# The first twenty microseconds of a two-layer decoder step: finer first loads, an earlier split of two weight units, a later norm, spare products

## The chip, the cores and the metric

The kernel runs on one core of one Trainium2 chip. A core has five engines that work side by side: TensorE multiplies matrices, VectorE (DVE in the profile) and ScalarE (ACT) do elementwise work, GpSimd (POOL) does elementwise work and starts DMAs, SyncE (SP) only starts DMAs. They meet through semaphores. SBUF is the memory on the core in which all tiles lie, PSUM the eight banks that TensorE writes. The metric is the device time of one execution in microseconds; the median of several executions is compared.

## The reference, cut to what matters

One step of a two-layer decoder trunk runs on 264 tokens (256 of a prompt, 8 samples). Only the beginning of layer 0 matters here:

```python
def rmsnorm(x, g):
    y = xf * lax.rsqrt(jnp.mean(xf * xf, axis=-1, keepdims=True) + NORM_EPS)
    return (y * g.astype(jnp.float32)).astype(x.dtype)
...
    z = jnp.einsum('bld,de->ble', hn, w_in)          # hn = rmsnorm(h, norm1), 1024 -> 2560
    u = z[..., :POOL_WIDTH]
    q, k, v, g = jnp.split(z[..., POOL_WIDTH:], 4, axis=-1)
    q = rope(...); k = rope(...) * (RET_HEAD_DIM ** -0.5)
```

After the two mixers follow an output projection, a feed-forward block (layer 0) or eight experts (layer 1), and a gated embedding.

## The kernel before, in words

**Operands in two parts.** Every fp32 product is made of three faster ones: an operand is split into a high part (rounded to the type fp32r, a copy by ScalarE) and a low part (the difference, by VectorE). `weights_first` issues xh*whi, xl*whi and xh*wlo (lines 727, 728, 729). So a weight "unit" (1024 rows x 256 columns, 1 MB, landing in the tile `raw`) must pass ScalarE (`hi`, line 1284, writes `whi`) and VectorE (`lo`, line 1575, writes `wlo`, in place of `raw`) before TensorE may use it. The input x (tile `h`, eight rows of 128 partitions x 264) passes ScalarE (`part`, line 1294: `xh`, scaled by the norm's gains) and VectorE (`finish`, line 1586: `xl`).

**Units and chunks.** w_in of layer 0 is ten units, numbered 0 to 9 (q, q, k, k, v, v, u, u, gate, gate). Each gives two "chunks" of 128 output columns, 24 products each, in a PSUM bank; chunk n is in bank n mod 4, banks 4 to 7 are for side steps. A chunk is scaled by the norm and taken out of PSUM by VectorE (`z_chunk`, lines 1721 and 1724), which counts `acc_free`; TensorE starts chunk n >= 4 only after `acc_free` has reached n - 3.

**The start.** Unit 0 comes in two halves (rows 0 to 511, 512 to 1023; line 661), unit 1 and unit 2 as a whole (line 649). `first_pair` runs a unit with both its chunks side by side, row block by row block, so that it can start with a part of the unit. The norm does not hold up the products: it is applied to the chunks afterwards. Its sum of squares is built from squares of x (five by GpSimd, line 2134, three by ScalarE, line 1460), four additions on GpSimd (line 2140) and four full fp32 products with a matrix of 1/1024 (line 869), which stand between the two halves of unit 1; then come a square root on ScalarE (line 1345) and a reciprocal on VectorE (line 1626).

**Order on the engines.** Each engine's program is written out by hand. `ahead(u)` splits unit u + 2 while unit u is multiplied. In layer 0 VectorE goes through j = 0 to 9 with: split of unit j + 2, then chunks 2j and 2j + 1.

**Rope.** As soon as chunk 3 (the last of q) has been taken out, GpSimd starts four DMAs that copy q with its halves swapped (line 2155, tile `sg`); the same for k after chunk 7 (tile `o`). After chunk 9 VectorE multiplies the swapped copy by the sine (line 1704) and adds (line 1706). The same for k follows chunk 11. After chunk 15 TensorE makes small side products, among them the scores of the retention (line 902), which VectorE scales (line 1644), and window sums for the samples (line 909); VectorE's rope steps, chunk copies and splits stand in its queue ahead of that scaling.

**Loads.** SP's queue carries the weights in the order of use; from unit 8 on a load waits until an older unit has been used (`unit_used`). Before that nothing holds the queue back. ScalarE's queue carries x (four DMAs, line 1448) and the 20 KB of gains ahead of it (line 1446).

## Time and profile before

| what | value |
|---|---|
| median of 3 executions | 892.67 us (892.07, 892.67, 894.69) |
| the profiled execution | 894.15 us, of which the span from first to last instruction is 892.4 us |
| TensorE busy | 869.1 us, 97% of the span |
| VectorE, ScalarE, GpSimd busy | 78%, 61%, 20% |
| granted TensorE clock, mean over the span | 0.993 |
| DMA | 237.59 MB, 266 GB/s |

Times in the rows further down are microseconds from the start of the span. The profiled execution lies 1.75 us above its span and inside the range of the three timed ones.

### The profile page before, as it was taken

To read this page: it belongs to the slowest core of one execution; us is meant where nothing else is said; L and a number is where in the kernel's file an instruction comes from. 1 tells how busy PE (TensorE), PEld (TensorE's weight loads), DVE (VectorE), ACT (ScalarE), POOL (GpSimd) and SP (SyncE) were. 2 spreads that over 40 slices of the span, in tenths; PEclk is the share of its full clock that TensorE was granted. 3 is DMA by queue.
4 is the path that set the end of the run, shared out by engine and by line. 5 is a ranking of instruction groups with operands and counts; after the bars stand their busy time and mean duration, and the time that the engine had idled before them with its cause. 6 is when DMAs were issued, how large, how long until landed. Compare 5 with 4: busy or idle time off the path is not lost.

```text
span 892.4 us, 14470 instructions
## 1 busy us (share of the span) xinstructions
PE 869.1 (97%) x5919; PEld 756.3 (85%) x5919; DVE 694.4 (78%) x797; ACT 541.2 (61%) x659; POOL 179.1 (20%) x190
## 2 busy tenths in 40 slices
PE   6999999999999999999999999999999999999995
PEld 6999899999999999999887777777777767777794
DVE  5796776564655588786869889898998989898976
ACT  5435654443435356355557878787778778876752
POOL 5456321100110012564411030003000100010012
PEclk9999999999999999999999999999999999999998
DMA  9993555545554554955339999999999999999801
GB/s 338 365 335 98 174 199 201 198 149 198 190 190 142 196 181 155 293 168 186 137 122 364 413 333 367 413 355 368 399 391 361 357 412 361 407 358 390 333 2 48
DMA packets 50739, 237.59 MB, mean 266 GB/s; under 512 B 4866, under 2 KB 8226, under 8 KB 42944
## 3 DMA queue, kind: packets, MB, share of 16 engines
q1 hardware_dynamic: 44672, 215.51, 64.7%
q0 software_dynamic: 5280, 20.04, 8.1%
q10 hardware_dynamic: 720, 1.10, 0.4%
q8 instruction: 47, 0.77, 0.3%
q14 instruction: 20, 0.16, 0.1%
HBM read 226.38 MB, written 9.63 MB: 264 GB/s over the span
## 4 chain that ended last, share of the span: by engine, by line
PE 78%; DVE 12%; ACT 4%; issue 3%; DMA 2%; POOL 1%; ACTq 0%; DVEq 0%; POOLq 0%
PE bank L727 12%; PE bank L728 11%; PE bank L729 11%; PE bank L1093 8%; PE bank L1094 8%; PE bank L1095 8%; DVE wlo L1575 5%; PE bank L1119 4%; PE bank L1118 4%; PE bank L1120 4%; ACT whi L1284 2%; DMA raw<-in_moe_w_down 1%; PE bank L854 1%; DMA o<-qk 1%; PE bank L1051 1%
## 5 line engine op out<-in xcount | busy, mean ns | idle before, releaser
L1575 DVE TENSOR_TENSOR wlo<-raw,whi 128x1408 fp32r<-128x1408 f32 (+2 forms) x292 | 466.9, 1633 | 96.1 <-ACT whi L1284 95.9
L1284 ACT ACTIVATE whi<-raw 128x1408 fp32r<-128x1408 f32 (+2 forms) x292 | 392.4, 1377 | 145.7 <-PE bank L729 82.3
L727 PE MATMUL bank<-xh,whi 128*128 128x264 f32 x672 | 194.6, 290 | 9.0 <-DVE xl L1586 8.2
L728 PE MATMUL bank<-xl,whi 128*128 128x264 f32 x672 | 192.3, 286 | 0.0
L729 PE MATMUL bank<-xh,wlo 128*128 128x264 f32 x672 | 192.1, 286 | 0.0
L1093 PE MATMUL bank<-whi,xeh 128*96 128x512 f32 (+1 forms) x384 | 143.8, 374 | 0.6 <-DVE hid L1879 0.6
L1094 PE MATMUL bank<-wlo,xeh 128*96 128x512 f32 (+1 forms) x384 | 143.6, 374 | 0.0
L1095 PE MATMUL bank<-whi,xel 128*96 128x512 f32 (+1 forms) x384 | 143.2, 373 | 0.0
L727 PEld LDWEIGHTS bank<-xh,whi 128*128 128x128 f32 x672 | 128.4, 191 | 10.4 <-DVE wlo L1966 8.2
L728 PEld LDWEIGHTS bank<-xl,whi 128*128 128x128 f32 x672 | 128.6, 191 | 0.1
L729 PEld LDWEIGHTS bank<-xh,wlo 128*128 128x128 f32 x672 | 127.9, 190 | 0.0
L1093 PEld LDWEIGHTS bank<-whi,xeh 128*96 128x96 f32 x384 | 62.0, 161 | 21.0 <-DVE wlo L1575 0.9
L1094 PEld LDWEIGHTS bank<-wlo,xeh 128*96 128x96 f32 x384 | 61.9, 161 | 19.1
L1095 PEld LDWEIGHTS bank<-whi,xel 128*96 128x96 f32 x384 | 61.8, 161 | 19.0
L727 PE MATMUL bank<-mh,whi 128*128 128x264 f32 x256 | 74.2, 290 | 0.6 <-DVE wlo L1575 0.5
L729 PE MATMUL bank<-mh,wlo 128*128 128x264 f32 x256 | 72.6, 284 | 0.0
L728 PE MATMUL bank<-ml,whi 128*128 128x264 f32 x256 | 72.6, 284 | 0.0
L1118 PE MATMUL bank<-whi,hh 128*96 128x512 f32 x176 | 70.4, 400 | 0.0
L1119 PE MATMUL bank<-wlo,hh 128*96 128x512 f32 x176 | 69.3, 394 | 0.0
L1120 PE MATMUL bank<-whi,hl 128*96 128x512 f32 x176 | 69.0, 392 | 0.0
L2110 POOL DMA_INDIRECT summed<-ys,to_row x6 | 8.7, 1456 | 225.6 <-ACT ys L1404 134.1
L727 PEld LDWEIGHTS bank<-mh,whi 128*128 128x128 f32 x256 | 48.2, 188 | 3.9 <-issue 1.9
(264 smaller groups left out, 1242.8 us busy)
## 6 DMA issues: line engine op xcount, KB each, us to landing
raw<-in_moe_w_gate SPq DMA_DIRECT2D x32, 1408.0 KB, 9.2
raw<-in_moe_w_up SPq DMA_DIRECT2D x32, 1408.0 KB, 9.5
raw<-in_moe_w_down SPq DMA_DIRECT2D x40, 1024.0 KB, 8.9
raw<-in_w_in SPq DMA_DIRECT2D x17, 1024.0 KB, 6.0
raw<-in_ffn_w_down SPq DMA_DIRECT2D x16, 704.0 KB, 4.2
raw<-in_ffn_w_gate SPq DMA_DIRECT2D x10, 1024.0 KB, 4.9
raw<-in_ffn_w_up SPq DMA_DIRECT2D x10, 1024.0 KB, 5.1
raw<-in_w_o SPq DMA_DIRECT2D x8, 1024.0 KB, 11.1
```

Of the source, the lines that this page charges most:

```text
L727: pe.matmul(out, w_hi, x_hi, start=start, stop=False)
L728: pe.matmul(out, w_hi, x_lo, start=False, stop=False)
L729: return pe.matmul(out, w_lo, x_hi, start=False, stop=stop)
L854: mm = pe.matmul(b[0:HD, a:a + 2], S[:, s, c, :], qm[:, s, c, :], start=True, stop=True)
L1093: pe.matmul(b, X, H[:, lo:lo + n], start=(k == 0), stop=False)
L1094: pe.matmul(b, X, L[:, lo:lo + n], start=False, stop=False)
L1095: mm = pe.matmul(b, Y, H[:, lo:lo + n], start=False, stop=(k == DC - 1))
L1118: pe.matmul(b, X, H[:, own], start=(i == 0), stop=False)
L1119: pe.matmul(b, X, L[:, own], start=False, stop=False)
L1120: mm = pe.matmul(b, Y, H[:, own], start=False, stop=(i == EC - 1))
L1284: act.activation(unit_hi(u), unit_raw(u), ACT.Copy).then_inc(hi_ready, 1)
L1575: dve.tensor_tensor(unit_lo(u), unit_raw(u), unit_hi(u).bitcast(F32), ALU.subtract).then_inc(lo_ready, 1)
```

## The change

It does the following, all of it in layer 0's first three units.

1. **Loads.** Unit 0 comes in quarters (two row blocks each), unit 1 in halves, on SP's queue. The gains move from the head of ScalarE's queue to the third place on SP's. x stays on ScalarE's queue, but its third and fourth DMA are issued after the loading of ScalarE's table and after the first quarter's high part. The load of unit 3 moves ahead of the large block of constants.
2. **Splits.** `hi_part` and `lo_part` split unit 0 by quarters and unit 1 by halves, each quarter ahead of the two rows of x that go with it. Units 2 and 3 are split right after unit 1: on ScalarE unit 2 ahead of six of the squares and unit 3 ahead of the square root, on VectorE both ahead of the reciprocal.
3. **Squares.** All eight are ScalarE's now; GpSimd only adds.
4. **Norm.** TensorE's four fp32 products of the norm move from the middle of unit 1 to the middle of unit 2 (between chunks 4 and 5).
5. **Banks.** Chunks 4, 5 and 6 go to banks 5, 6 and 7, and only from chunk 7 on does TensorE wait for `acc_free`.
6. **Spare products.** At the head of its program TensorE makes five full fp32 products of a tile of zeros into bank 7, 128 x 264 each, once that tile has been cleared; nobody reads them.

```diff
+        def main_bank(n):
+            return n + 1 if n in (4, 5, 6) else n % 4
...
-            first_rows(0, top_in)
-            first_rows(1, raw_landed[0])
+            first_rows(0, 0, top_in[0])
+            first_rows(0, 1, top_in[1])
+            sp.dma_start(gains[:, :, :], t["gains"]).then_inc(gains_in, 16)
+            first_rows(0, 2, top_in[2])
+            first_rows(0, 3, raw_landed[0])
+            first_rows(1, 0, top_in[3])
+            first_rows(1, 1, raw_landed[1])
+            load_rows(2, t["w_in_rows"][:, 512:768])
             sp.dma_start(const[:, 0:FIRST_CONST], t["const"][:, 0:FIRST_CONST]).then_inc(first_in, 16)
-            for u in range(1, 3):
-                load_rows(u, t["w_in_rows"][:, 256 * u:256 * (u + 1)])
+            dense(0, U_MIX[0] + 3, W_IN[3:4])
             sp.dma_start(const[:, FIRST_CONST:], t["const"][:, FIRST_CONST:]).then_inc(const_in, 16)
...
-                if at >= 4:
+                if at >= 7:
                     pe.wait_ge(acc_free, n - 3)
-                out = bank[at % 4][:, 0:T]
+                out = bank[main_bank(at)][:, 0:T]
...
-                if between is not None:
+                if between == (0, FIRST_NORM_IN):
+                    side_step(0, "norm1")
+                elif between is not None:
...
-                    if u and half == 0:
-                        side_step(0, "norm1")
...
+            pe.wait_ge(still, 1)
+            for _ in range(5):
+                pe.matmul(bank[7][:, 0:T], sq[:, 0, 0:P], sq[:, 0, :], start=True, stop=True)
...
-            act.dma_start(gains[:, :, :], t["gains"]).then_inc(gains_in, 16)
...
+            fetch_x(0)
+            fetch_x(1)
             act.wait_ge(still, 1)
             act.activation(rstd[0:1, 0:1], sq[0:1, 0, 0:1], ACT.Sqrt)
+            fetch_x(2)
+            for i in range(4):
+                hi_part(0, i)
+                if i == 0:
+                    fetch_x(3)
+                for m in (2 * i, 2 * i + 1):
+                    h_final(act, 0, m)
+                    part(0, m)
+            for m in range(2):
+                first_square(m)
+            for i in range(2):
+                hi_part(1, i)
+            ahead(0)
+            for m in range(2, DC):
+                first_square(m)
+            ahead(1)
...
+            for i in range(4):
+                lo_part(0, i)
+                for m in (2 * i, 2 * i + 1):
+                    finish(0, m)
+            for i in range(2):
+                lo_part(1, i)
+            ahead(0)
+            ahead(1)
...
-            for m in range(5):
-                pool.wait_ge(x_in[m // 2], 16)
-                pool.tensor_tensor(first[:, m, :], h[:, m, :], h[:, m, :], ALU.mult).then_inc(pool_step, 1)
-                steps += 1
-            pool.wait_ge(pool_step, steps)
             for m in range(0, DC, 2):
-                if m >= 4:
-                    pool.wait_ge(first_sq, m // 2 * 2 - 3)
+                pool.wait_ge(first_sq, m + 2)
```

How the order moves, at three places. First SP's queue at the start of the program, before and after (`raw` is the weights' landing tile, 128x4x256 a half of a unit, 128x2x256 a quarter, 128x8x256 a whole one):

```order
L661 DMA raw<-in_w_in_rows 128x4x256 x2
L686 DMA const<-in_const 128x129
L649 DMA raw<-in_w_in_rows 128x8x256 x2
L689 DMA const<-in_const 128x2709
L690 DMA pscale<-in_pscale 128x8
```

```order
L667 DMA raw<-in_w_in_rows 128x2x256 x2
L692 DMA gains<-in_gains 128x40
L667 DMA raw<-in_w_in_rows 128x2x256 x2
L667 DMA raw<-in_w_in_rows 128x4x256 x2
L655 DMA raw<-in_w_in_rows 128x8x256
L698 DMA const<-in_const 128x129
L645 DMA raw<-in_w_in 128x2048
L700 DMA const<-in_const 128x2709
```

The gains now follow two quarters; ahead of unit 2 (line 655) stand the same weights as before, without the first constants.

Second ScalarE at its first square root and the splits around it, before and after (line 1443, then 1463, is the high part of a piece of unit 0 or 1, line 1284, then 1303, of a whole unit; `first` holds the squares):

```order
L1443 ACTIVATE whi<-raw 128x1024 [waits raw_landed1] x2
L1460 ACTIVATE first<-h 128x264 x3
L1284 ACTIVATE whi<-raw 128x2048 [waits raw_landed2]
L1345 ACTIVATE rstd<-bank,const 128x264 [waits side_full,first_in]
L1284 ACTIVATE whi<-raw 128x2048 [waits unit_used,raw_landed3]
```

```order
L1468 ACTIVATE first<-h 128x264 x2
L1463 ACTIVATE whi<-raw 128x1024 [waits top_in3]
L1463 ACTIVATE whi<-raw 128x1024 [waits raw_landed1]
L1303 ACTIVATE whi<-raw 128x2048 [waits raw_landed2]
L1468 ACTIVATE first<-h 128x264 x6
L1303 ACTIVATE whi<-raw 128x2048 [waits unit_used,raw_landed3]
L1364 ACTIVATE rstd<-bank,const 128x264 [waits side_full,first_in]
```

Six squares now stand behind the split of unit 2, and the split of unit 3 has moved ahead of the square root.

Third VectorE around the reciprocal, before and after (line 1575, then 1609, is the low part of a unit; the rows `qk<-bank,rstd` are the chunks of q and k):

```order
L1575 TENSOR_TENSOR wlo<-raw,whi 128x2048 [waits hi_ready]
L1626 RECIPROCAL rstd<-rstd 128x264 [waits std_ready]
L1724 TENSOR_TENSOR qk<-bank,rstd 128x264 [waits acc_full,side_free]
L1724 TENSOR_TENSOR qk<-bank,rstd 128x264 [waits unit_used]
L1575 TENSOR_TENSOR wlo<-raw,whi 128x2048 [waits hi_ready]
L1724 TENSOR_TENSOR qk<-bank,rstd 128x264 [waits acc_full]
L1724 TENSOR_TENSOR qk<-bank,rstd 128x264 [waits unit_used]
```

```order
L1609 TENSOR_TENSOR wlo<-raw,whi 128x2048 [waits hi_ready] x2
L1660 RECIPROCAL rstd<-rstd 128x264 [waits std_ready]
L1758 TENSOR_TENSOR qk<-bank,rstd 128x264 [waits acc_full,side_free]
L1758 TENSOR_TENSOR qk<-bank,rstd 128x264 [waits unit_used]
L1758 TENSOR_TENSOR qk<-bank,rstd 128x264 [waits acc_full]
L1758 TENSOR_TENSOR qk<-bank,rstd 128x264 [waits unit_used]
```

The low part of unit 3 has moved from between chunks 1 and 2 to ahead of the reciprocal.

## Rows read from the trace of the kernel before

**Rows 1.** The page, busy time, share of the span and instructions of each engine

```profile
PE 869.1 (97%) x5919; PEld 756.3 (85%) x5919; DVE 694.4 (78%) x797; ACT 541.2 (61%) x659; POOL 179.1 (20%) x190
```

**Rows 2.** TensorE's waits over the whole span: total us, times, longest

```profile
PE bank L909 <- DVE sc L1644: 0.5, 1, 0.5
```

**Rows 3.** Timeline of the start: start us, us, engine, line, operation, [idle before <-releaser]

```profile
0.75 0.32 POOL L2131 MEMSET sq<- 128x264 f32 x1 [0.29 <-POOLq L2297]
0.76 1.01 SPq L661 DMA_DIRECT2D raw<-in_w_in_rows  x2
...
4.83 1.06 ACT L1443 ACTIVATE whi<-raw 128x1024 fp32r<-128x1024 f32 x1
...
5.79 0.90 ACT L1294 ACTIVATE xh<-h,gains 128x264 fp32r<-128x264 f32 x2
5.92 1.41 DVE L1966 TENSOR_TENSOR wlo<-raw,whi 128x1024 fp32r<-128x1024 f32 x1 [5.92 <-ACT whi L1443]
7.25 1.62 DVE L1586 SCALAR_TENSOR_TENSOR xl<-h,gains,xh 128x264 fp32r<-128x264 f32 x2
...
8.24 0.56 PE L727 MATMUL bank<-xh,whi 128*128 128x264 f32 x1 [8.24 <-DVE xl L1586]
```

**Rows 4.** Stretches: busy us (count) by engine, then granted clock, DMA share, GB/s

```profile
8.20:13.40 5.20, 5.11 (x21) 4.84 (x22) 5.14 (x7) 4.17 (x9) 4.43 (x5) 1.00 1.08 354
...
71.50:74.80 3.30, 3.30 (x16) 3.30 (x17) 0.33 (x2) 2.75 (x7) 2.99 (x5) 0.52 0.00 0
```

**Rows 5.** Timeline of TensorE where its products become shorter

```profile
13.41 0.37 PE L727 MATMUL bank<-xh,whi 128*128 128x264 f32 x1
13.62 0.28 PE L728 MATMUL bank<-xl,whi 128*128 128x264 f32 x1
13.74 0.28 PE L729 MATMUL bank<-xh,wlo 128*128 128x264 f32 x1
```

**Rows 6.** DMA issues of the first 40 us: KB each, median us from issue to landing

```profile
raw<-in_w_in_rows SPq DMA_DIRECT2D x2, 512.0 KB, 5.3
...
const<-in_const SPq DMA_DIRECT2D x1, 64.5 KB, 7.0
```

**Rows 7.** Line 649, the loads of units 1 and 2: issue times, then times to landing

```profile
L649 SPq DMA_DIRECT2D raw<-in_w_in_rows x2: 657/1312/1966, 2.4 to 3.1; - x2
...
DMA to landing us min/median/max: 10.0/11.1/12.3
```

**Rows 8.** Timeline of VectorE: the low part of unit 2; `xl` late, GpSimd idle

```profile
17.28 2.69 DVE L1575 TENSOR_TENSOR wlo<-raw,whi 128x2048 fp32r<-128x2048 f32 x1 [0.79 <-ACT whi L1284]
...
119.48 0.48 DVE L1586 SCALAR_TENSOR_TENSOR xl<-h,gains,xh 128x264 fp32r<-128x264 f32 x1
```

**Rows 9.** Timeline from the norm's products to the start of unit 3

```profile
19.70 1.94 PE L869 MATMUL bank<-first,const 128*128 128x264 f32 x8
21.28 0.48 PE L727 MATMUL bank<-xh,whi 128*128 128x264 f32 x1
...
22.25 1.80 DVE L1626 RECIPROCAL rstd<-rstd 128x264 f32<-128x264 f32 x1 [2.28 <-ACT rstd L1345]
...
24.67 0.36 PE L727 MATMUL bank<-xh,whi 128*128 128x264 f32 x1
...
26.98 0.77 DVE L1724 TENSOR_TENSOR qk<-bank,rstd 128x264 f32<-128x264 f32 x2
...
30.55 0.28 PE L727 MATMUL bank<-xh,whi 128*128 128x264 f32 x1
```

**Rows 10.** Timeline: the swap of q on GpSimd's queue, VectorE's sine product

```profile
28.41 2.19 POOL L2155 DMA_DIRECT2D sg<-qk  x4 [9.71 <-DVE qk L1724]
...
42.70 2.84 DVE L1704 TENSOR_TENSOR sg<-sg,const 128x1056 f32<-128x1056 f32 x1
```

**Rows 11.** Line 2155, the last two of q's four swaps, time to landing

```profile
DMA to landing us min/median/max: 8.2/8.8/9.4
```

**Rows 12.** A stretch from chunk 9 to VectorE's last rope step, columns as in rows 4

```profile
42.30:62.50 20.20, 20.20 (x177) 19.84 (x176) 20.04 (x21) 7.19 (x6) 10.04 (x7) 1.00 0.97 333
```

More of the change, by code:

```diff
@@ L506, in program @@
         hi_ready, lo_ready, unit_used = sem("hi_ready"), sem("lo_ready"), sem("unit_used")
[L508 removed]
+        x_in, gains_in, top_in = [sem(f"x_in{i}") for i in range(4)], sem("gains_in"), [sem(f"top_in{i}") for i in range(4)]
         first_in, const_in, layer_in = sem("first_in"), sem("const_in"), sem("layer_in")
@@ L653, in dense, with first_rows @@
                     load(first + j, t[name][layer][:, n * c0:n * (c0 + w)], n * w)
-            def first_rows(half, landed):
-                _, _, n, _, w = W_IN[0]
-                n //= 2
-                dst = unit_half(raw, 0, half).rearrange("p (k w) -> p k w", k=n)
-                src = t["w_in_rows"][half * n * P:(half + 1) * n * P, 0:w]
+            def first_rows(u, part, landed):
+                _, _, n, _, w = W_IN[u]
+                n //= FIRST_PARTS[u]
+                dst = unit_part(raw, u, part).rearrange("p (k w) -> p k w", k=n)
+                src = t["w_in_rows"][part * n * P:(part + 1) * n * P, u * w:(u + 1) * w]
                 sp.dma_start(dst, src.rearrange("(k p) w -> p k w", p=P)).then_inc(landed, 16)
@@ L764, in first_pair @@
                 L = unit_lo(u).rearrange("p (k w) -> p k w", k=DC)
-                for half in range(2):
-                    pe.wait_ge(lo_ready if half else first_lo, u + 1)
-                    for k in range(4 * half, 4 * half + 4):
+                parts = FIRST_PARTS[u]
+                rows = DC // parts
+                for part in range(parts):
+                    if part == parts - 1:
+                        pe.wait_ge(lo_ready, u + 1)
+                    else:
+                        pe.wait_ge(first_lo, u * (FIRST_PARTS[0] - 1) + part + 1)
+                    for k in range(rows * part, rows * (part + 1)):
                         if u == 0:
@@ L1212, in _ @@
                     if j > 1:
-                        unit_pair(U_MIX[l] + j, A_MIX[l] + 2 * j, xh, xl, between=(l, j) if j in AMID else None)
+                        unit_pair(U_MIX[l] + j, A_MIX[l] + 2 * j, xh, xl, between=(l, j) if j in AMID or (l, j) == (0, FIRST_NORM_IN) else None)
                     elif l == 0:
@@ L1961, in over_expert, with lo_part @@
                     dve.tensor_tensor(h[:, m, :], h[:, m, :], osg[:, :], ALU.add).then_inc(o_done, 1)
-            def lo_half(u, half):
-                dve.wait_ge(hi_ready if half else first_hi, u + 1)
-                dve.tensor_tensor(unit_half(wlo, u, half), unit_half(raw, u, half), unit_half(whi, u, half, HIGH_AT).bitcast(F32),
-                                  ALU.subtract).then_inc(lo_ready if half else first_lo, 1)
-            lo_half(0, 0)
-            for m in range(DC):
-                finish(0, m)
-                if m == 1:
-                    lo_half(0, 1)
-            for half in range(2):
-                lo_half(1, half)
+            def lo_part(u, part):
+                last = part == FIRST_PARTS[u] - 1
+                if last:
+                    dve.wait_ge(hi_ready, u + 1)
+                else:
+                    dve.wait_ge(first_hi, u * (FIRST_PARTS[0] - 1) + part + 1)
+                dve.tensor_tensor(unit_part(wlo, u, part), unit_part(raw, u, part), unit_part(whi, u, part, HIGH_AT).bitcast(F32),
+                                  ALU.subtract).then_inc(lo_ready if last else first_lo, 1)
+            for i in range(4):
[6 more added lines that the diff above has]
+            ahead(1)
             for l in range(DEPTH):
                 for j in range(10):
-                    ahead(U_MIX[l] + j)
+                    if l or j >= 2:
+                        ahead(U_MIX[l] + j)
                     if j == 0:
```

41 lines of the change are left out of this document (18 added, 23 removed).

## The prediction, made before the changed kernel was run

> **What bounds the kernel now.** I read the page's busy line first: TensorE is busy 869.1 of 892.4 us [rows 1]. So there are two kinds of gain: a shorter stretch in which it has nothing to do, and a stretch in which its products are longer than they need be. Its waits come next. The one large idle time is the start: the first product comes at 8.24, behind VectorE's first low parts [rows 3]. Every other wait is small; the largest in layer 0's mixer is 0.5 us on VectorE's scaled scores, line 1644 [rows 2]. Third, the timeline of its products: the one at 13.41 starts 0.21 us ahead of its successor, the one at 13.62 only 0.12, and so it stays [rows 5]. That is the low level of TensorE's clock, 1.2 GHz, against 2.4. The granted-clock column says 1.00 for 8.2 to 13.4, but the 21 products there fill 5.2 us, just as 16 fill 3.3 us in the one later stretch where the column says 0.52 [rows 4]; so I trust the spacing. The low clock costs some 22 products x 0.10 = 2.2 us at the start, and 16 x 0.10 = 1.6 us at 71.5.
>
> Last, what else is full: the DMA engines carry 0.97 to 1.08 of their time at the start and from 42 to 62 [rows 4, 12], and VectorE is busy 20.04 of 20.2 us from chunk 9 to the last rope step [rows 12]. Both decide how much of an earlier start survives.
>
> **First products.** The first half of unit 0, issued at 0.76, was in at 4.83, when ScalarE took it [rows 3]. Two quarters are the same bytes. The gains now stand right behind them, and ScalarE can't make its first `xh` without them. No row shows them there. Below: with the two quarters, 4.83. Above: the 64.5 KB of constants, queued at 1.8 behind both halves, took 7.0 us [rows 6], which is 8.8. The halves took 5.3 us at the median of the two [rows 6], 4.1 and so 6.5: the second, issued at 1.3, was in at 7.8, the constants 1.0 later. So I take 4.83 + 1.0 = 5.85. One `xh` and one `xl` of 0.5 each follow (0.48 for `xl` when GpSimd is idle [rows 8]) and 0.14 to start: first product at 7.0, 1.25 earlier than 8.24.
>
> **Unit 0.** VectorE needs per quarter a low part of 512 columns and two `xl`. Before, GpSimd squared x at the same time and the costs were 1.41 for 1024 columns and 0.81 for one `xl` [rows 3]; now GpSimd is idle there, so I take 0.65 + 2 x 0.48 = 1.6, with 0.7 + 1.62 = 2.3 as the upper bound. The last `xl` is done at 6.35 + 2 x 0.48 + 3 x 1.6 = 12.1, and TensorE ends unit 0 at 12.9. At the high clock TensorE alone would need 7.0 + 48 x 0.12 = 12.8, so it just keeps step.
>
> Five spare products run from about 1.1, when the tile has been cleared [rows 3]. The norm's four fp32 products take 1.94 us at the high clock [rows 9], so five take 2.4, or 4.8 at the low one: to about 5.9. They hide in the idle start; if they ran on past 7.0 they would push unit 0 by the excess. What they can save is the low stretch: all 2.2 us, or nothing. I take it that the clock is up during unit 0, since it rose 5.2 us after work began and their work begins 5.9 us ahead of the first product.
>
> The Trainium skill (TensorE: Matmul & The Clock Gate, Part 1) says that the low level is the default, that activity lifts it, and that the moment varies from run to run because the monitor does not start with the kernel. The trace agrees with the first two: low at the start, up at 13.41, down once more at 71.5. By its third statement the spare products may miss in some executions; that is the rival "clock stays low".
>
> **Unit 1.** It was landed at 2.35 + 10.0 = 12.35 [rows 7]. Halves, and 64.5 KB less ahead of them, make it a little earlier. ScalarE needs 0.9 for a pair of `xh` and 0.53 for a quarter [rows 3]: 5.85 + 0.9 + 3 x 1.43 = 11.05, two squares to 11.95 (taken like a pair of `xh`), the halves at 12.95 and 13.95. VectorE's first low half is done 1.25 later, at 14.2. TensorE: 14.2 + 48 x 0.12 = 20.0.
>
> **Unit 2.** Its bytes stand behind the same weights and x as before, on full DMA engines, so I leave its landing at 3.05 + 12.3 = 15.35 [rows 7]. High part to 17.28, low part 2.69: 19.97, as in the row of before [rows 8]. GpSimd added at the same time, as it still does; undisturbed the low part may be shorter. So chunk 4 starts at 20.0, when unit 1 ends too, 4.7 us ahead of the 24.67 of before [rows 9]. No bank holds it: chunks 4 to 6 have their own. Before, unit 1's second half ended at 21.5 + 24 x 0.12 = 24.4, so that wait was 0.3 us.
>
> **The norm** costs the same wherever it stands: 19.70 to 21.5 is 1.8 us [rows 9] (the next record, at 21.28, is 0.2 longer than its kind). The six squares behind unit 2's high part end at 17.28 + 6 x 0.45 = 20.0; GpSimd's last addition, even at twice a disturbed `xl`, ends by 21.6, and the products need it at 22.9: hidden, by 1.3 us. Chunk 4 to 22.9, norm to 24.7, chunk 5 to 27.6. Chunk 6 began at 30.55 [rows 9]. TensorE is **2.95 us** ahead there.
>
> **What is late next.** The norm now ends at 24.7, before at 21.5. From it to the reciprocal are 0.75 us, the reciprocal is 1.80, four chunks go out in 2 x 0.77 without the split between them: 28.8. Before, chunk 3 was out at 26.98 + 0.77 = 27.75 [rows 9]. So the swap of q, which started 0.66 later at 28.41 [rows 10], starts at 29.45, **1.04 later**. Its last DMA, issued at 30.1, landed 9.4 us later [rows 11]: 39.5; now 40.55. VectorE's sine product needs both this and chunk 9. It began at 42.70 [rows 10], right behind chunk 9, with 3.2 us to spare for the swap; now chunk 9 is out at 42.70 - 2.95 = 39.75 and the swap decides: 40.55, 2.15 earlier than before. From there VectorE has no free time for 20 us, and TensorE waits on it at line 909. So 2.95 shrinks to **2.15**. The swap of k waits for chunk 7, and stays in step.
>
> **The sum** for the profiled execution: 894.15 - 2.15 = 892.0. The rest follows TensorE (loads wait for used units), so the shift stays to the end. The profiled execution lies above the median of 892.67. Part of the spread is when the clock rises; executions of before in which it rises sooner have less to gain. Half of a possible 0.8 us, my choice, goes off: 892.67 - (2.15 - 0.4) = **890.9**.
>
> **Rivals.**
> - *The whole shift survives*: the swap of q takes 0.8 us less, for instance because SP's queue is emptier by then. Against it: full DMA engines. 892.67 - 2.55 = 890.1.
> - *Clock stays low*: as before for 5.2 us from the first product, 7.0 to 12.2, which is 24 products; 24 more to 15.1; unit 1 ends at 20.9 rather than 20.0. Shift 2.15 - 0.9 = 1.25: 891.4.
> - *The gains come late, and the kernel is slower*: at 8.8, the upper bound. ScalarE stands at its first `xh` with everything behind it, so all its work, unit 1's and unit 2's high parts included, is later: by 2.95: first product 9.95, unit 1 through at 22.95 (unit 2's low part at 21.5 no longer counts), norm 25.85 to 27.65, swap of q at 32.4 and landed at 43.5, 0.8 later than 42.70. Against the median: 892.67 + 0.8 + 0.4 = 893.9. It decides from a landing of about 7.6 on. For it: full DMA engines; against it: they stand behind two quarters, not behind four.
>
> **Chances.** The forecast 0.55 (own range 889.8 to 892.0), whole shift 0.22, clock low 0.13, gains late 0.10. Range 889.0 to 893.0: it leaves out most of the last rival and, below, a shift above 3.7, which unit 2's landing forbids. A measurement of this kernel tells about 0.3%, 2.7 us, from no change. Faster by more than that (below 890.0) takes half of the second case and the lower third of the first: 0.30; slower 0.04; within 0.66.
>
> **What would show it.** First product near 7.0, and 0.12 us apart within unit 0; gains landing near 5.9, ahead of the third quarter; unit 2's low part done near 20.0 with chunk 4 right behind it; norm's products at 22.9; chunk 6 near 27.6; the swap of q near 29.4, and VectorE idle ahead of the sine product with the DMA as releaser. I'd be wrong if unit 2 landed far from 15.35, since everything from chunk 4 on hangs on it, if VectorE's `xl` stayed at 0.8, or if the swap of q took another 9.4 us but chunk 9 were not waiting for it.

## The result: slower by half a per cent, and the profile after

The changed kernel takes 897.29 us (median of 6 executions, 896.39 to 898.97), the kernel before 892.65 in the same series. The ratio, taken over all executions and so not quite that of the medians, is **1.0047** with an interval of 1.0033 to 1.0061, so 2.9 to 5.4 us slower. The prediction was 890.9. The profiled execution took 897.28 us, its span 895.4.

The page's busy line of the changed kernel, which answers to [rows 1]. TensorE is busy 5.3 us more than before, while the span grew by 3.0; the spare products, 4.7 us of it, were idle time before.

```profile
PE 874.4 (98%) x5929; PEld 759.3 (85%) x5929; DVE 692.7 (77%) x799; ACT 542.8 (61%) x666; POOL 176.7 (20%) x185
```

The timeline of its start, which answers to [rows 3, 5]:

```profile
1.12 4.70 PE L1226 MATMUL bank<-sq 128*128 128x264 f32 x10 [1.12 <-POOL sq L2171]
1.77 0.46 SPq L692 DMA_DIRECT2D gains<-in_gains  x1
...
7.00 0.92 ACT L1313 ACTIVATE xh<-h,gains 128x264 fp32r<-128x264 f32 x2 [1.77 <-DMA gains<-in_gains]
...
8.18 0.36 PE L738 MATMUL bank<-xh,whi 128*128 128x264 f32 x1 [2.36 <-DVE xl L1620]
8.38 0.28 PE L739 MATMUL bank<-xl,whi 128*128 128x264 f32 x1
...
8.98 0.37 PE L738 MATMUL bank<-xh,whi 128*128 128x264 f32 x1
9.15 0.42 PE L739 MATMUL bank<-xl,whi 128*128 128x264 f32 x1
9.37 0.42 PE L740 MATMUL bank<-xh,wlo 128*128 128x264 f32 x1
```

ScalarE waits 1.77 us for the gains, the first product comes at 8.18 (before: 8.24), and the products are 0.12 us apart only until 8.98; then 0.22 until 12.23. From 8.18 to the norm's products at 24.45 no wait of TensorE is listed: 120 products fill it.

From the norm to the sine product, which answers to [rows 9, 10]:

```profile
24.45 1.94 PE L885 MATMUL bank<-first,const 128*128 128x264 f32 x8
27.01 1.80 DVE L1660 RECIPROCAL rstd<-rstd 128x264 f32<-128x264 f32 x1 [3.56 <-ACT rstd L1364]
28.84 1.45 DVE L1758 TENSOR_TENSOR qk<-bank,rstd 128x264 f32<-128x264 f32 x4
29.14 0.28 PE L738 MATMUL bank<-xh,whi 128*128 128x264 f32 x1
...
30.96 2.17 POOL L2189 DMA_DIRECT2D sg<-qk  x4 [8.78 <-DVE qk L1758]
40.94 0.43 DVE L1758 TENSOR_TENSOR v<-bank,rstd 128x264 f32<-128x264 f32 x1 [1.15 <-PE bank L740]
43.33 2.45 POOL L2200 TENSOR_TENSOR qk<-qk,const 128x1056 f32<-128x1056 f32 x1 [2.35 <-DMA sg<-qk]
43.35 3.55 DVE L1738 TENSOR_TENSOR sg<-sg,const 128x1056 f32<-128x1056 f32 x1 [1.98 <-DMA sg<-qk]
```

Chunk 6 starts at 29.14, 1.41 us ahead of before, and chunk 9 (line 1758 at 40.94) is 1.41 ahead too. But VectorE then stands for 1.98 us until the swap of q has landed, and its sine product takes 3.55 us instead of 2.84. It ends at 46.90; before at 45.54.

The same stretch before, with GpSimd's cosine product, chunk 9, VectorE's scaled scores and TensorE's window sums behind them:

```profile
41.91 2.49 POOL L2166 TENSOR_TENSOR qk<-qk,const 128x1056 f32<-128x1056 f32 x1
42.35 0.43 DVE L1724 TENSOR_TENSOR v<-bank,rstd 128x264 f32<-128x264 f32 x1 [1.15 <-PE bank L729]
...
62.48 1.28 DVE L1644 TENSOR_TENSOR sc<-bank,const 128x512 f32<-128x512 f32 x2
63.22 1.06 PE L909 MATMUL bank<-const,buf 120*128 120x8 f32 x8
```

The last two of q's four swaps in the changed kernel, from issue to landing (their flight), against [rows 11]; then the scaled scores, and TensorE's longest wait in the mixer, against [rows 2]:

```profile
DMA to landing us min/median/max: 9.2/9.9/10.6
```

```profile
63.61 1.28 DVE L1678 TENSOR_TENSOR sc<-bank,const 128x512 f32<-128x512 f32 x2
64.34 1.88 PE L925 MATMUL bank<-const,buf 120*128 120x8 f32 x8 [2.61 <-DVE sc L1678]
```

```profile
PE bank L925 <- DVE sc L1678: 3.1, 2, 2.6
```

The 0.5 us of [rows 2] lies at 392 us, in layer 1. In layer 0 of the kernel before no wait at the window sums is listed: TensorE was through with the work ahead of them at 63.14 and began them at 63.22, as the scores came.

Stretches of the start and of that wait (busy us and count of PE, PEld, DVE, ACT, POOL; granted clock; DMA share; GB/s):

```profile
8.00:12.00 4.00, 3.82 (x20) 3.85 (x21) 3.97 (x10) 4.00 (x10) 0.00 (x0) 0.63 1.08 356
...
60.00:64.00 4.00, 1.73 (x22) 1.37 (x18) 4.00 (x6) 2.06 (x4) 0.21 (x1) 0.96 0.89 333
64.00:68.00 4.00, 3.66 (x24) 3.36 (x24) 2.27 (x5) 2.30 (x2) 2.80 (x6) 0.50 0.36 105
68.00:72.00 4.00, 4.00 (x32) 3.72 (x31) 2.48 (x4) 1.74 (x8) 3.61 (x6) 0.69 0.70 166
```

The scaled scores start at 63.61, 1.13 later than the 62.48 of before. TensorE stands for 2.6 us until they come, and its clock is at the low level from 63.6 to 70.5 (granted clock 0.51); before, it was there from 71.6 to 75.0 (0.50). Against the kernel before, the same work is 1.12 us late at the window sums and 2.36 late at 94 us, and it stays so up to 450 us. So the time is not lost in the start, where TensorE was ahead, but where VectorE's chain is met again, and behind it.

### The profile page after: what moved, and what is told of

It is laid out like the page before. It is cut to its first block, busy times and chain, and to the rows that moved or that the text cites. A ratio compares the mean times of both kernels' runs of the same rounds, so it can differ in the third digit from the quotient of the medians.

```text
span 895.4 us, 14497 instructions
## 1 busy us (share of the span) xinstructions
PE 874.4 (98%) x5929; PEld 759.3 (85%) x5929; DVE 692.7 (77%) x799; ACT 542.8 (61%) x666; POOL 176.7 (20%) x185
## 4 chain that ended last, share of the span: by engine, by line
PE 74%; DVE 12%; DMA 5%; ACT 4%; issue 3%; POOL 1%; SPq 0%; ACTq 0%; DVEq 0%; POOLq 0%
PE bank L738 11%; PE bank L739 10%; PE bank L740 10%; PE bank L1109 8%; PE bank L1110 8%; PE bank L1111 8%; DVE wlo L1609 5%; PE bank L1135 4%; PE bank L1134 4%; PE bank L1136 4%; ACT whi L1303 2%; DMA xt<-summed 1%; DMA sg<-qk 1%; DMA summed<-ys,to_row 1%; PE bank L870 1%
## 5 line engine op out<-in xcount | busy, mean ns | idle before, releaser
L1109 PEld LDWEIGHTS bank<-whi,xeh 128*96 128x96 f32 x384 | 61.9, 161 | 21.5 <-DVE wlo L1609 1.5
```

The costliest lines, as they stand in the source:

```text
L1109: pe.matmul(b, X, H[:, lo:lo + n], start=(k == 0), stop=False)
```

## The experiments

All were timed against the kernel before on the same chip; its medians there were 892.65, 893.85, 893.59, 894.03 and 893.97 us in the five series. "Swap" is the start of q's four DMAs on GpSimd's queue, "scores" the start of VectorE's scaled scores in layer 0, "wait" TensorE's wait for them there ("none": none is listed), all of one profiled execution each. "Clock" is the mean granted clock over all executions of the kernel (6 to 12; 106 of before). It covers the whole span, also the last 6 to 9 us, in which TensorE has next to nothing left to do and the clock is low in every profile.

| kernel | swap | sine starts | scores | wait | clock | median us | ratio (95% interval) |
|---|---|---|---|---|---|---|---|
| before | 28.41 | 42.70 | 62.48 | none | .9938 | | 1 |
| before, second profile | 27.95 | 42.24 | 62.15 | 0.2 | | | |
| the change | 30.96 | 43.35 | 63.61 | 2.6 | .9898 | 897.29 | 1.0047 (1.0033 to 1.0061) |
| e1 gains first | 29.41 | 42.54 | 62.81 | 3.2 | .9924 | 896.01 | 1.0028 (1.0017 to 1.0039) |
| e2 early norm | 27.45 | 41.41 | 60.99 | none | .9924 | 894.40 | 1.0008 (.9997 to 1.0018) |
| e3 late norm alone | 30.91 | 43.01 | 63.29 | 2.3 | .9913 | 897.87 | 1.0048 (1.0031 to 1.0065) |
| e4 filled wait | 31.92 | 44.81 | 65.08 | 0.9 | .9922 | 897.26 | 1.0032 (1.0019 to 1.0046) |
| e5 = e1 + e2 | 26.79 | 40.69 | 60.28 | none | .9938 | 892.96 | .9992 (.9978 to 1.0006) |
| e6 = e5, no spares | 27.07 | 41.04 | 60.93 | 0.2 | .9924 | 892.87 | .9992 (.9979 to 1.0006) |
| e8 weights held | 30.14 | 42.97 | 63.87 | 2.1 | .9923 | 896.80 | 1.0032 (1.0018 to 1.0046) |
| e9 k held | 29.52 | 41.53 | 66.82 | 3.1 | .9908 | 901.31 | 1.0078 (1.0059 to 1.0097) |
| e10 low part first | 30.01 | 44.26 | 62.31 | 2.3 | .9923 | 895.92 | 1.0024 (1.0007 to 1.0042) |
| e11 wait put into before | 28.86 | 43.15 | 65.63 | 2.8 | .9920 | 897.57 | 1.0039 (1.0028 to 1.0051) |
| e12 = e11, filled | 27.92 | 42.20 | 63.94 | none | .9938 | 896.31 | 1.0037 (1.0023 to 1.0050) |
| e13 norm between units | 26.22 | 40.07 | 60.62 | 0.8 | .9943 | 893.44 | .9995 (.9984 to 1.0006) |
| e14 = e13, no spares | 26.50 | 40.35 | 60.02 | none | .9938 | 892.41 | .9987 (.9972 to 1.0003) |
| e15 = e13, swap late | 33.94 | 46.89 | 67.12 | 0.9 | .9903 | 902.83 | 1.0086 (1.0065 to 1.0107) |

### Which part costs the time: e1, e2, e3

My theory after the result: the late norm delays q's swap, the swap holds VectorE, and VectorE holds TensorE at the window sums. The rival was the prediction's own, that late gains cost it.

**e1** puts the gains back at the head of ScalarE's queue.

```diff
-            sp.dma_start(gains[:, :, :], t["gains"]).then_inc(gains_in, 16)
...
+            act.dma_start(gains[:, :, :], t["gains"]).then_inc(gains_in, 16)
             fetch_x(0)
```

> The changed kernel with the gains back at the head of ScalarE's queue; all else as changed. Theory 'late swap' (the norm now ends in the middle of unit 2, so the swap of q lands late, VectorE's chain to the scaled scores is late and TensorE waits 2.6 us for it): the first product moves from 8.18 to about 6.8, norm and swap follow by 1.0 to 1.4, but the wait at the window sums (2.6 us) stays within 0.5 us of what it was, so the time falls by only about 1.2, to 896. Rival 'late gains' (the gains at 7.00 instead of 5.85 are what turned the gain into a loss): the wait falls below 0.8 us and the time is at or below that of the kernel before, 891 to 893.

Its timeline, then the landing of q's last two swaps:

```profile
5.95 0.56 PE L737 MATMUL bank<-xh,whi 128*128 128x264 f32 x1
...
29.41 2.18 POOL L2189 DMA_DIRECT2D sg<-qk  x4 [6.80 <-DVE qk L1758]
39.37 0.43 DVE L1758 TENSOR_TENSOR v<-bank,rstd 128x264 f32<-128x264 f32 x1 [1.15 <-PE bank L739]
42.52 2.46 POOL L2200 TENSOR_TENSOR qk<-qk,const 128x1056 f32<-128x1056 f32 x1 [3.10 <-DMA sg<-qk]
42.54 3.55 DVE L1738 TENSOR_TENSOR sg<-sg,const 128x1056 f32<-128x1056 f32 x1 [2.73 <-DMA sg<-qk]
```

```profile
DMA to landing us min/median/max: 9.6/10.5/11.4
```

The first product is 2.23 us earlier than in the change, chunk 9 is out at 39.80, 2.98 ahead of before, and the kernel is still slower, at the 896 that the theory expected. The wait, 3.2, grew by 0.6 instead of staying within 0.5. The gains account for 1.55 us at the swap and 0.80 at the scores, no more. Up to chunk 9 this is the prediction's plan, carried out; the loss stands behind it. Not all of it is at the scores, which are only 0.33 late: in e1's profile the work is 0.34 late at 450 us too, and 1.6 late from 500 to 700 us, behind a wait of TensorE for ScalarE (1.1 us, line 1108) that before does not have.

**e2** is the change with the norm as before: in the middle of unit 1, five squares on GpSimd, units 2 and 3 split at their old places.

```diff
-                if between == (0, FIRST_NORM_IN):
-                    side_step(0, "norm1")
-                elif between is not None:
+                if between is not None:
...
+                    if u and part == 0:
+                        side_step(0, "norm1")
```

> The changed kernel with the norm back between the halves of unit 1, five squares back on GpSimd and the splits of units 2 and 3 back in their old order; quarters, gains on the second place, banks and spare products stay. Theory 'late swap': the swap of q starts at or before 28.4 (30.96 in the changed kernel), it lands by 41, TensorE's wait for the scaled scores is under 1 us (2.6), and the time is 891 to 892.5. Rival 'late gains': the first product is still at 8.2 and the time stays at 896 to 898. Rival 'clock at the start' (the spare products make the clock fall during unit 0): it stays at 896 to 898 too.

Its timeline:

```profile
27.45 2.20 POOL L2187 DMA_DIRECT2D sg<-qk  x4 [8.96 <-DVE qk L1753]
...
41.41 2.84 DVE L1733 TENSOR_TENSOR sg<-sg,const 128x1056 f32<-128x1056 f32 x1
```

The sine product stands right behind chunk 9 again, without idle time and with its old length, no wait at the window sums is listed, and the loss is gone (1.0008). It is not the gain that was expected, though: 894.40 against 891 to 892.5.

**e3** goes the other way: the kernel before with the late norm, its squares, splits and banks, and nothing else of the change.

```diff
+                if between == (0, FIRST_NORM_IN):
+                    side_step(0, "norm1")
...
-                    if u and half == 0:
-                        side_step(0, "norm1")
```

> The kernel before with only the late norm (middle of unit 2, own banks for chunks 4 to 6, all squares on ScalarE, units 2 and 3 split ahead); halves, gains and no spare products as before. Theory 'late swap': unit 1 ends near 22.8, the norm near 27.3, the swap of q starts near 32.3 and lands near 44.0, VectorE's sine product is 1.3 later than 42.70, TensorE waits about 1.8 us for the scaled scores; with the clock falling behind that wait the time is 894 to 896. Rival 'late gains' or 'clock at the start': 892.6, no change, since neither is in it.

Its timeline:

```profile
30.91 2.17 POOL L2162 DMA_DIRECT2D sg<-qk  x4 [8.21 <-DVE qk L1734]
...
43.01 3.56 DVE L1714 TENSOR_TENSOR sg<-sg,const 128x1056 f32<-128x1056 f32 x1 [1.69 <-DMA sg<-qk]
```

The ratio is 1.0048, that of the whole change 1.0047: the late norm, with the squares, splits and banks that go with it, is enough for the loss. (e13 below keeps squares and banks and has no loss.) The swap came earlier than expected, at 30.91 and not near 32.3, and the time is above the 894 to 896.

**The second profile of before** tells how far two executions of one kernel differ.

> The kernel before, unchanged, for a second profile of it. In its first profile the experts' stage (404 to 494 us) is 1.0 to 1.3 us shorter than in the profiles of the kernels with early gains or with the norm back. Theory 'that is spread of one execution': here the stage is longer than in the first profile, by 0.5 us or more. Rival 'the change costs there': within 0.3 us of the first.

The experts' stage is 1.6 us longer here, as the theory said, but by a fall of the clock at 408.0 to 411.4 (0.50). The clock's fall behind 71.5, which [rows 4] shows, isn't there. Stretches of it:

```profile
68.00:72.00 4.00, 4.00 (x49) 3.84 (x48) 2.49 (x4) 3.64 (x16) 3.77 (x4) 1.00 0.23 55
72.00:76.00 4.00, 4.00 (x58) 3.77 (x57) 1.05 (x3) 3.28 (x6) 3.76 (x4) 1.00 0.24 41
```

It is 1.9 us ahead of the first profile at 76 to 400 us and only 0.2 to 0.3 ahead from 415 to 700 us. So a difference of 2 us at one place, in one profile, is no evidence. The wait for ScalarE that e1 has near 490 us is in neither profile of before, but e12, which starts like before, has 0.8 us of it and e4, with the whole change, none: the theory of spread fits, and no run tests it further.

### What is left with the norm early: e5, e6

**e5** is e1 and e2 together; **e6** takes the five spare products out of e5.

```diff
-            for _ in range(5):
-                pe.matmul(bank[7][:, 0:T], sq[:, 0, 0:P], sq[:, 0, :], start=True, stop=True)
```

> Both undone together: the gains back at the head of ScalarE's queue, and the norm, the squares and the split order back as before; quarters, halves, own banks, load order and spare products stay. Theory 'late swap': with the early gains TensorE is about 3 us ahead at chunk 9 (out near 39.4), and now the swap of q starts by 27 and lands by 38.5, so VectorE's sine product starts at chunk 9's end near 39.5, the scaled scores come near 59.3 (62.48 before), TensorE waits no more than 0.5 us there, and the kernel is faster than the one before by 1.5 to 3 us (ratio 0.9967 to 0.9985). Rival 'a lead at the start is given back anyway' (the experts' stage, bound by loads, takes it): the scaled scores come near 59.3 all the same, and the ratio is 0.9995 to 1.001.

> The same without the five spare products at the start. Theory 'the spare products lift the clock ahead of the real ones': the products of unit 0 are 0.22 us apart for up to 5 us from 5.95 on, TensorE is 1.0 to 2.0 us later at chunk 9 than with them (near 41), and the time is higher by 1 to 2 us. Rival 'they do nothing': product spacing, chunk 9 and time within 0.3 us of the kernel with them.

The scores are 2.2 us earlier in e5 than in before, and the ratio is .9992 with 1 in its interval: the gain of 1.5 to 3 us did not come, and the rival's range holds it. In e5's profile 1.6 of the 2.2 us are gone at 94 us, behind low stretches of the clock at 70.2 to 73.6 and 80.4 to 83.8, where before has one. The spare products change the spacing (e6: 0.22 from 6.37 to 8.57; e5: 0.12) but nothing in the time: the two kernels have the same ratio.

### Why the swap lands late: e8, e9, e10

In e1 the last swap flew 11.4 us, before 9.4. The candidates were the weights that share the DMA engines, and the swap of k, which follows q's by 5.4 us now and followed by 8.9.

**e8** is e1 with the load of the output weights held until q's swap has landed; **e9** is e1 with k's swap, and what is queued behind it on GpSimd, held until then.

```diff
+            sp.wait_ge(swapped[0], 64)
             dense(0, U_WO[0], W_O)
```

```diff
+                    if l == 0 and a == 1:
+                        pool.wait_ge(swapped[0], 64)
```

> The changed kernel with the gains early (late norm as in the change), and the first load of the output weights, issued at 27.8 there, held back on SyncE's queue until the swap of q has landed. Theory 'the swap flies 11.4 us because weights share the DMA engines with it': the last of q's four DMAs lands 9.4 us or less after its issue at 31.1, so near 40.5 rather than 42.5; VectorE's chain is 2 us earlier, TensorE's wait for the scaled scores falls from 3.2 to near 1.2, and the time falls by 1.5 to 2 us, to a ratio near 1.0005. Rival 'the flight does not depend on that load' (what flies was queued earlier): landing within 0.5 us of 42.5, time unchanged, ratio near 1.0028.

> The changed kernel with early gains (late norm), and GpSimd starts the swap of k, and the state loads behind it, only once the swap of q has landed. Theory 'q's swap flies long because k's swap and the states follow it after 5.4 us, where they followed after 8.9 before': the last of q's DMAs lands 9.4 us after its issue at 31.1, near 40.5 instead of 42.5, and VectorE's first sine product starts there; k's swap then lands near 51, so the scaled scores gain at most 1 us and the time stays within 1 us of the kernel without the hold (ratio 1.002 to 1.003). Rival 'the flight is set by what was queued before it': q still lands within 0.4 us of 42.5, k near 53, and the time rises by 2 us or more.

In e8 the last flight is 11.1 us: a miss, this load isn't it. In e9 it is 10.2. But e3, in which k's swap is not held, has 10.3, so e9 does not show k's swap to be the reason. The three last flights of e9, then of e3:

```profile
DMA to landing us min/median/max: 8.3/9.4/10.2
```

```profile
DMA to landing us min/median/max: 6.9/9.0/10.3
```

All seven profiles with the norm in the middle of unit 2 have a last flight of 10.2 to 11.4 us; the nine in which the swap starts earlier, at 26.2 to 28.9 us, have 9.1 to 9.6. So the longer flight goes with the later start; what in it does it is not shown. As a kernel e9 is far slower, a miss too, and its timeline says why:

```profile
41.53 1.26 DVE L1738 TENSOR_TENSOR sg<-sg,const 128x1056 f32<-128x1056 f32 x1 [1.62 <-DMA sg<-qk]
...
49.22 1.26 DVE L1740 TENSOR_TENSOR qk<-qk,sg 128x1056 f32<-128x1056 f32 x1 [6.43 <-POOL qk L2202]
```

GpSimd's cosine product now stands behind the issues of k's swap, so VectorE's addition waits 6.43 us for it. But the sine product, with no cosine beside it, takes 1.26 us. That gives the three lengths: 1.26 alone, 2.84 where the cosine began 0.8 us ahead of it (before), 3.55 where both began with the landing of one swap (e1, the change, e3). What the rows have in common is the end: in every run in which the two overlap, for q and for k, the sine ends 1.1 us behind the cosine.

**e10** is e1 with VectorE's low part of unit 7 ahead of the sine product, to fill the time it waits for the swap.

```diff
+                    if l == 0 and j == 5:
+                        rope(l, 0)
...
-                        rope(l, ROPE_AFTER[j])
+                        if l or j != 4:
+                            rope(l, ROPE_AFTER[j])
```

> The changed kernel with early gains (late norm), and VectorE makes the low part of unit 7 ahead of the first sine product instead of behind it, into the 2.7 us in which it waits for the swap of q. Theory 'late swap': the sine product starts near 43.6 (42.54), the scaled scores come near 61.6 (62.81), TensorE's wait there falls from 3.2 to about 2.0, and the time falls by about 1.2, to a ratio of 1.0014. Rival 'VectorE's chain does not decide': the scaled scores come earlier but the ratio stays at 1.0028.

VectorE still stands for 1.65 us, now ahead of the low part, for its high part; the scores come 0.5 us earlier, and 1.0024 can't be told from e1's 1.0028. In its profile the norm was 0.6 us later than in e1's, so this run decides nothing.

### What the wait costs beside itself: e4, e11, e12

**e4** is the change with five more spare products of TensorE ahead of the window sums, so that it has work during its wait.

```diff
+                if (l, name) == (0, "win"):
+                    pe.wait_ge(const_in, 64)
+                    pe.wait_ge(acc_free, 13)
+                    for _ in range(5):
+                        pe.matmul(bank[0][:, 0:T], ident, const[:, 0:T], start=True, stop=True)
```

> The changed kernel plus five spare full fp32 products (about 2.4 us in all) on TensorE in the place where it waits 2.6 us for the scaled scores; nobody reads them. Theory 'the wait also costs clock': the wait keeps its end at 64.3, but the window sums behind it take 1.0 us rather than 1.9, the granted clock of 64 to 68 is near 1.0 rather than 0.50, and the time falls by about 1.2, to 896.1, or by nothing if the clock then falls at 71.5 as it does in the kernel before. Rival 'the clock falls for another reason': granted clock and time as in the changed kernel, 897.3.

Its clock was 1.00 in 64 to 68 us, but .57 in 68 to 72, and low once more from 85.3 to 88.7: the fall was put off, not avoided. Inconclusive.

**e11** puts a wait of the same size into the kernel before, where no swap is late: VectorE makes one product of its chain four times. **e12** is e11 with e4's filling.

```diff
+                        for _ in range(0 if l else 3):
+                            step(dve.tensor_tensor(qxi[:, :, :], qk[:, 0, :, CH:2 * CH], xi, ALU.mult))
```

> The kernel before with one small product of VectorE (line 1997, 0.6 us) made four times instead of once, ahead of the scaled scores; nothing else is changed. TensorE's wait for the scaled scores grows from 0.5 to about 2.5 us. Theory 'the wait also costs clock': behind it the granted clock is near 0.5 for some us, and the time grows by 2.0 plus 1.0 to 1.6, to a ratio of 1.0034 to 1.0040. Rival 'the wait costs itself alone': ratio 1.0022. Rival 'TensorE's wait there is hidden': 1.0.

> The same, with five spare full fp32 products (2.4 us) on TensorE in that wait. The scaled scores come when they came without them. Theory 'the wait also costs clock': the clock stays up behind the place, and the time is 1.0 to 1.6 us lower than without the spare products, ratio near 1.0022. Rival 'the clock falls anyway in this stage, only at another place' (as it did at 68 to 72 in the changed kernel with the wait filled): time as without them.

Stretches of e11, then of e12:

```profile
64.00:68.00 4.00, 1.64 (x8) 1.64 (x8) 4.00 (x7) 3.01 (x3) 3.77 (x7) 0.70 1.02 316
68.00:72.00 4.00, 4.00 (x34) 3.51 (x33) 0.98 (x3) 2.71 (x12) 3.58 (x6) 0.50 0.51 122
```

```profile
64.00:68.00 4.00, 4.00 (x45) 3.40 (x45) 3.28 (x8) 0.59 (x1) 3.60 (x7) 1.00 1.01 281
68.00:72.00 4.00, 4.00 (x43) 3.86 (x43) 3.80 (x4) 3.90 (x16) 3.79 (x3) 1.00 0.24 55
```

2.13 us of VectorE's work, with no other edit, makes the kernel slower by .0028 to .0051: VectorE's chain decides here. With the wait filled the clock stays up at this place; it is low from 82.9 to 86.3 instead of 65.6 to 72.4 (mean .9938 instead of .9920; times 893 us that is 1.6 us of low clock). Yet the ratios, 1.0039 and 1.0037, can't be told apart, and e12's swap was 0.9 us earlier than e11's, with no edit ahead of it. So the earlier fall of the clock is shown, its price is not shown by these two. What the record does show is that the two go together: over the 255 timed executions of all kernels here, one whose mean clock is .001 below its kernel's mean takes 0.6 us longer on average (correlation -0.66). That is no proof of the direction, and the mean holds the idle end of the kernel too.

### The norm in between, and the swap alone: e13, e14, e15

**e13** is e1 with all squares ahead of unit 2's split on ScalarE, the norm's products between units 1 and 2, and VectorE's low part of unit 3 behind chunks 0 to 3. **e14** is e13 without the spare products (e6's edit).

```diff
+                        if j == 1:
+                            side_step(0, "norm1")
...
-            ahead(0)
             for m in range(2, DC):
                 first_square(m)
+            ahead(0)
             ahead(1)
...
+                    if l == 0 and j == 1:
+                        ahead(U_MIX[0] + 1)
```

**e15** is e13 with one number changed, so that GpSimd starts q's swap later.

```diff
-                    pool.wait_ge(acc_free, A_MIX[l] + 4 * a + 4)
+                    pool.wait_ge(acc_free, A_MIX[l] + (4 * a + 4 if l or a else 7))
```

> The changed kernel with early gains, all squares on ScalarE ahead of unit 2's split, the norm between units 1 and 2, and the low part of unit 3 behind chunks 0 to 3. Theory 'late swap': norm from about 19.8 to 21.4, reciprocal 21.9 to 23.7, swap of q from 25.8 and landed by 36, chunk 9 out near 39.3 and the sine product right behind it, scaled scores near 59.1 (62.48 before), no wait over 0.5 us at the window sums, time 2 to 3.4 us below the kernel before (ratio 0.9962 to 0.9978). Rival 'a lead is given back later': the same times up to the window sums, ratio 0.999 to 1.0005.

> The same without the five spare products. Theory 'spare products save the low stretch of the clock': unit 0's products are 0.22 us apart for some 5 us from 6.0 on, chunk 9 is 0.5 to 1.5 us later, the time 0.5 to 1.5 us higher. Rival 'VectorE sets the pace of unit 0 anyway': chunk 9 and time within 0.3 us of those with spare products.

> The kernel with the norm between units 1 and 2, where GpSimd starts the swap of q only once chunk 6 has been taken out, instead of chunk 3; nothing else is changed. Theory 'late swap': q's swap starts near 31.2 (30.96 in the changed kernel), lands at 42.5 to 43.3, VectorE waits 3 us or more for it, the scaled scores come at 62.8 to 63.6, TensorE waits some 3.5 us for them, the clock falls behind that wait, and the time is 4 to 6 us above the kernel with the early swap, a ratio of 1.001 to 1.004 to the kernel before. Rival 'the swap's landing is hidden': scaled scores and time within 0.5 us of the kernel with the early swap.

The timeline of e13, then of e15:

```profile
26.22 2.18 POOL L2190 DMA_DIRECT2D sg<-qk  x4 [8.42 <-DVE qk L1758]
...
40.07 2.84 DVE L1738 TENSOR_TENSOR sg<-sg,const 128x1056 f32<-128x1056 f32 x1
```

```profile
33.94 2.16 POOL L2190 DMA_DIRECT2D sg<-qk  x4 [16.03 <-DVE qk L1755]
36.09 1.94 POOL L2190 DMA_DIRECT2D o<-qk  x4
...
46.89 3.57 DVE L1738 TENSOR_TENSOR sg<-sg,const 128x1056 f32<-128x1056 f32 x1 [6.64 <-DMA sg<-qk]
```

The gain of 2 to 3.4 us that was expected of e13 did not show: .9995 lies in the rival's range. And e14 is not slower than e13, as its theory said; its sine product, right behind chunk 9, starts 0.28 us later, as the rival said.

In e15 the swap was to start at about 31.2 and started at 33.94, for the chunk that it now waits for stood behind more work than I had counted. The direction is all the clearer: with the start of the program untouched, a swap 7.7 us later makes the scores 6.5 us later and the kernel 9.4 us slower than e13 by the medians (902.83 against 893.44; expected were 4 to 6), 4.5 by the two profiled executions (897.73 against 893.22). TensorE's long wait was not for the scores, as I had expected, but ahead of them, for VectorE's copy of v, which stands in the queue behind the sine product:

```profile
PE bank L906 <- DVE v L1758: 3.4, 1, 3.4
```

The clock has its part again: two of the six executions, with a mean of .993, take 897.7 and 898.0 us, the four with .989 take 902.4 to 903.7; .004 of 893 is 3.6 us.

## Why the prediction was wrong

By its own steps:

- **First products: wrong in size.** The gains landed at 7.0, not 5.85, 5.2 us after their issue behind two quarters of 256 KB. e1 shows what that was worth: 0.8 us at the scores. The rival "gains late" had the right sign and the right place (the swap of q), but not the cause: with the gains early the ratio is still 1.0028.
- **Unit 0: half right.** VectorE's quarter took 1.41 us, a little less than the 1.6 forecast. The spare products lifted the clock, but it fell back at 8.98, after TensorE had stood for 2.36 us, so it was low for 15 products and 1.5 us. With the gains early it is up from the first product in e13 (0.12 apart from 5.90) and from 6.75 in e1, but TensorE then waits for its operands instead, and e13 and e14, e5 and e6 can't be told apart in time: the low clock at the start hid a wait.
- **Units 1 and 2, the norm: right in kind, late by the gains and the clock.** Unit 2's low part, on which I had hung chunk 4, was done at 19.25 (forecast 20.0) and held up nothing; TensorE itself came to chunk 4 only at 21.5. Chunk 5 was to begin at 24.7 and did at 26.04, chunk 6 at 29.14 instead of 27.6. In e1 they fit: the swap starts at 29.41, forecast 29.45; chunk 9 is out at 39.80, forecast 39.75. A little luck is in it: e1's first product is 1.05 ahead of the forecast, but unit 1 had to wait for its low part until 14.05 (forecast 14.2).
- **What is late next: the step that failed**, in its words "the swap decides: 40.55, 2.15 earlier than before". I moved the start of the swap and kept its flight, 9.4 us, and the length of the sine product. In e1, with the start as forecast, the last flight is 11.4 and the sine product starts at 42.54, 2.0 late; and it takes 3.55 instead of 2.84, 0.7 more. Instead of 2.15 us early the scores were 0.33 late. Both count for the same reason: the swap had been hidden behind chunk 9, with 3.2 us to spare, and now decided. Why the flight grew stays open. The sine grew since GpSimd's cosine, which rewrites the tile that the swap reads, was let go at the same moment as the sine. The Trainium skill (SBUF — State Buffer, SBUF: two separate sides) says that a VectorE operation with two SBUF inputs and a GpSimd operation that reads SBUF take a shared pair of ports as an exclusive lock for a whole instruction. The trace agrees: in e1 the cosine ends at 44.98 and the sine 1.1 us behind it, at 46.09; before, 44.40 and 45.54; alone the sine takes 1.26.
- **"TensorE waits on it at line 909": unpriced.** The shift at chunk 9 was 1.41 us ahead; at the scores it was 1.13 behind. I had line 909 as a place where VectorE decides, read the 0.5 us of [rows 2] as layer 0's, and priced nothing for a wait there. Now there is one, of 2.6 us, and the granted clock is low from 63.6 to 70.5. Each profile of before has one low stretch half as long between its start and its end (71.6 to 75.0; 408.0 to 411.4). Half of the additional 3.5 us, my estimate of the loss, is 1.7; with 1.1 to 1.5 us later scores (against the first and the second profile) that makes 2.8 to 3.2, at the lower end of the measured 2.9 to 5.4.
- **"The shift stays to the end": nearly right.** From 94 to 450 us the change is 2.36 to 2.38 us late against the first profile; from 500 to 700 it is 2.8.
- **The range and the chances**: [rows 11] hold the last two of q's swaps alone; among k's four, the same copies on the same line, before had one of 10.3 us. I took the one number 9.4 and gave it no upper end. Even 10.3 would have been too little for e1's 11.4. The rival on the slower side was tied to the gains alone and got 0.10.

**Still open.** The longer flight: in e9, with k's swap held, it is 10.2, in e3 without that 10.3. VectorE's low parts beside the swap aren't the reason, as e13 has two of them back to back there and flies 9.4 us. Then some 2 us of the kernels with the new start, an estimate from two of them: e10's scores come when those of before do, e2's 1.2 to 1.5 us earlier, and neither is faster than before (1.0024 and 1.0008). And e14's gain: its scores are 2.46 us early and its profiled execution keeps the lead (2.4 us at 94 us, a span of 889.5 against 892.4), but its median is only 1.2 to 1.6 us lower than that of before, and its interval (.9972 to 1.0003) still holds 1. It is the best of these kernels, but not shown to beat the one before.

## What to carry to other kernels

An earlier product was worth nothing here, where another engine's chain is met again later; follow the step that is moved back (here a norm of 1.8 us) to the transfer it releases, and price that transfer's flight by no less than the slowest row of its kind once it is no longer hidden. When a wait moves, look at what else it lets go at the same moment: two operations that used to start apart may now start together and collide for longer. And do not count the clock's low stretch at a start as a loss before you have seen that operands would be there for faster products.

## What the runs showed of the hardware

- **VectorE beside GpSimd has a price of a factor of 2 to 3**: the same sine product of 128x1056 takes 1.26 us alone and 2.79 to 3.57 beside GpSimd's cosine, and in every overlap, q's and k's, it ends 1.1 us behind the cosine.
- **The granted clock fell around single waits in a kernel that is 97% busy**: 2.36 us at the start (0.63 from 8 to 12), 2.6 us at the window sums (0.50 from 64 to 68). With e1, e3, e8, e9 and e11 there are six profiles with a wait of 2.1 to 3.2 us at the window sums and a fall within 2 us of its end; after 2.3 us in e10's profile it did not fall. It fell without such a wait too: in before at 71.6, in e14 at 78.8, both times behind 32 products of 128x2 that took 2.03 us; in before's second profile the same products passed without one. The Trainium skill (TensorE: Matmul & The Clock Gate, Part 1) says that the low level returns after idleness, and that the moment of the rise varies from run to run. The rows agree with the second (13.6 and 12.2 us in the two profiles of before), and with the first for the six waits, not for the falls at 71.6 and 78.8.
- **The column of the granted clock is not to be trusted at the very start**: 1.00 in [rows 4] with products 0.22 apart, 0.63 in the change from 8 to 12, with the same spacing from 8.98.
- **20 KB took 5.2 us** on SyncE's queue behind two quarters, while ahead of x on ScalarE's queue they let the first product start at 5.95.
